# Two-layer RWKV-7 / neighbourhood-attention / retention step on one core: the next head pair's projections placed in the tail of a pair, its 64x64 inversion products on all four quadrants of TensorE

## What is computed

```python
h = rmsnorm(x, norm_mix_pre) * (1 + sc1) + sh1
z = h @ w_in                                   # 50 column tiles of 128; 40 of them belong to the head pairs
z_rwkv = dwconv3(z[..., :o0], rwkv_conv)       # three-tap convolution over time
r, k, v, wl, al, gl = split(z_rwkv)
kk = k * k_k;  kk = kk / max(sqrt(sum(kk * kk)), 1e-12)
decay = exp(-exp(w_log));  a = sigmoid(a0 + al @ a_up)
k_d = k * (1 + (a - 1) * k_a)
for t:                                         # both directions, per head
    S = S * w_t + (S a_t) b_t^T + v_t k_t^T;  y_t = S r_t
bonus = sum(r * k * r_k) * v
o = (head_groupnorm(y) * ln_g + ln_b + bonus) * g;  out_a = o @ w_o_rwkv
out_b = attention(q, k, v) @ w_o_na            # dense for the context, 8 x 16 neighbourhood for the latents
out_c = (head_groupnorm(retention(q, k, v)) * gn * silu(g)) @ w_o_ret
x = x + g1 * rmsnorm((gates * [out_a, out_b, out_c]).sum() @ w_out)
x = x + g2 * rmsnorm(conv_ffn(...))
```

## Time and profile before

| quantity | value |
|---|---|
| median of 3 runs | 2028.66 us (2023.75 to 2029.55) |
| the profiled execution's own time | 2028.39 us |
| its span | 2026.2 us |
| mean granted TensorE clock | 0.979 |
| busy: TensorE, VectorE, ScalarE, GpSimd | 93%, 50%, 46%, 47% |
| period of a pair (pair 1 to pair 2, layer 0) | 110.9 us |

### The profile page before, as it was taken

How to read it: one execution, slowest core, us unless ns; L and a number is a source line. 1 busy time by engine, 2 the same in 40 slices (tenths; PEclk the granted TensorE clock), 3 DMA queues, 4 the chain that set the end, 5 groups by cost and what they waited for, 6 DMA issues and landing times.

```text
span 2026.2 us, 41588 instructions
## 1 busy us (share of the span) xinstructions
PE 1890.5 (93%) x17864; PEld 1707.3 (84%) x17864; DVE 1005.3 (50%) x1516; ACT 939.4 (46%) x1766; POOL 942.6 (47%) x767
## 2 busy tenths in 40 slices
PE   5899999999999889999978999999999997999997
PEld 1887878787999779999948788787879996999996
DVE  3574756475612355551156566574655133455502
ACT  4554645454533454443355455453554334544432
POOL 1434435160666536666426052433516664466663
PEclk8999999999999989999989999999999999999998
DMA  7314142332443323334353241414224332234342
GB/s 291 104 53 147 55 133 79 111 102 88 136 125 125 104 73 124 121 123 126 132 214 107 62 131 55 136 55 135 77 98 147 124 125 83 94 125 125 125 125 73
DMA packets 65414, 231.52 MB, mean 114 GB/s; under 512 B 7376, under 2 KB 11856, under 8 KB 64592
## 3 DMA queue, kind: packets, MB, share of 16 engines
q1 hardware_dynamic: 59040, 215.21, 32.7%
q10 hardware_dynamic: 6192, 13.66, 1.9%
HBM read 223.58 MB, written 5.26 MB: 113 GB/s over the span
## 4 chain that ended last, share of the span: by engine, by line
PE 78%; DVE 11%; ACT 4%; issue 3%; POOL 2%; DMA 2%; ACTq 0%; SPq 0%; DVEq 0%; POOLq 0%
PE psz L471 55%; PE psw L471 20%; DVE work L1353 3%; ACT work L947 3%; DMA ring<-in_w 2%; DVE work L1362 2%; POOL ringlo L1728 1%; DVE part L1353 1%; PE psz L479 1%; ACT whi L947 1%; PE psw L479 1%; DVE rstd L1362 1%; DVE work L1356 1%; POOL work L1764 1%; DVE work L1359 0%
## 5 line engine op out<-in xcount | busy, mean ns | idle before, releaser
L1728 POOL TENSOR_TENSOR ringlo<-ring,whi 128x512 fp32r<-128x512 f32 x608 | 809.7, 1355 | 755.6 <-ACT whi L947 755.6
L471 PE MATMUL psz<-hhi,whi 128*128 128x386 f32 x1696 | 587.2, 346 | 23.2 <-POOL ringlo L1728 14.6
L471 PE MATMUL psz<-hlo,whi 128*128 128x386 f32 x1696 | 577.5, 340 | 0.0
L471 PE MATMUL psz<-hhi,ringlo 128*128 128x386 f32 x1696 | 576.3, 340 | 0.0
L947 ACT ACTIVATE whi<-ring 128x1024 fp32r<-128x1024 f32 x304 | 320.1, 1053 | 134.1 <-PE psz L471 125.7
L471 PE MATMUL psw<-work 64*64 64x64 f32 (+4 forms) x9024 | 347.5, 231 | 17.5 <-issue 9.0
L471 PEld LDWEIGHTS psw<-work 64*64 64x64 f32 (+2 forms) x9024 | 293.4, 136 | 72.1 <-issue 54.4
L471 PEld LDWEIGHTS psz<-hhi,whi 128*128 128x128 f32 x1696 | 320.9, 189 | 36.0 <-issue 18.6
L471 PE MATMUL psz<-part,whi 128*128 128x386 f32 x1344 | 346.6, 339 | 3.8 <-DVE work L1353 1.7
L471 PEld LDWEIGHTS psz<-hlo,whi 128*128 128x128 f32 x1696 | 322.9, 190 | 2.1
L471 PEld LDWEIGHTS psz<-hhi,ringlo 128*128 128x128 f32 x1696 | 321.1, 189 | 0.0
(11 more groups left out here) (105 smaller groups left out, 1700.6 us busy)
## 6 DMA issues: line engine op xcount, KB each, us to landing
ring<-in_w SPq DMA_DIRECT2D x400, 512.0 KB, 3.5
pk<-in_pk ACTq DMA_DIRECT2D x8, 832.0 KB, 4.5
const<-in_const SPq DMA_DIRECT2D x1, 1795.0 KB, 9.9
work<-in_x SPq DMA_DIRECT2D x1, 1544.0 KB, 6.8
work<-in_x ACTq DMA_DIRECT2D x1, 1544.0 KB, 9.0
out_x<-work ACTq DMA_DIRECT2D x1, 1544.0 KB, 5.6
work<-out_x ACTq DMA_DIRECT2D x1, 1544.0 KB, 8.8
out_x<-work SPq DMA_DIRECT2D x4, 386.0 KB, 2.4
```

The costliest lines, as they stand in the source:

```text
L471: ins = nc.tensor.matmul(out, a, b, start=start, stop=stop, skip_group_check=True)
L1728: L.do(G.tensor_tensor(out, a, b, op), S[sig] if sig else None)
```

## The change

What moves: the tiles r, k and v of pair p+1 are computed inside pair p (`next_steps`), 24 steps of three matmuls in eight groups from behind `wm`/`u` to the end of the pair. The stream of blocks in memory is the same; `ada_steps` moves forward, 14 of its 16 steps into levels 4 and 5. VectorE's `taps` of the next r, k, v and the new `key_tiles` follow in the tail, and `key_sums` opens the next pair, with nq behind it, then the low-rank products, nk, nv, rq. VectorE does `scale_rwkv` behind the scan of d = 0, `scale_ret` behind that of d = 1, and `finish` and the bonus behind the d-loop. GpSimd's `low` for rq and rk move into the loop's d = 0, behind `Lx` and behind the copies `pend`. The pair's parameters are loaded in two pieces (`load_ups`, `load_pack`). `Lx` and `Pi` get other buffers; `Px` holds the key norm.

In the levels hb = 1 takes the two other quadrants: its chunk operands `tvv`, `gg`, `g0`, `art` lie in the other half of the partitions, the loops run x outside and hb inside, and the waits ask for both heads. For it VectorE's transpose becomes one of 128 x 384 and two of 64 x 384 (`across`), and ScalarE's copy of `art` becomes three pieces.

```diff
-                        for i in range(p == 0, 5):
-                            dense(zb + i, bb + i)
+                        def next_steps(n):
+                            if p + 1 == PAIRS:
+                                return
+                            for _ in range(n):
+                                i, k = divmod(ahead[0], KT)
+                                zi, j = zb + ZI["r"] + i, bb + 10 + i
+                                if k == 0:
+                                    opened(zi)
+                                    pe.wait_ge(*after("w_lo", 2 * j + 2))
+                                three(z(zi), j, k, hsp[k], k == 0, k == KT - 1, "z_done" if k == KT - 1 else None)
+                                ahead[0] += 1
...
+                        else:
+                            key_sums()
+                            dense(zb + ZI["nq"], bb + 3)
                             pe.wait_ge(*at_of("yroot_ready", p - 1, 0))
                             pe.wait_ge(*at_of("rroot_ready", p - 1, 0))
+                            lora_up()
+                            dense(zb + ZI["nk"], bb + 4)
...
-                                    mm(psw[hc(c), hb, CH * x:CH * x + CH], au[hc(c), hb, x, 1, 0:CH],
+                                    mm(psw[hc(c ^ hb), hb, CH * x:CH * x + CH], au[hc(c), hb, x, 1, 0:CH],
...
-                                if lv == LEVELS - 1:
-                                    ada_steps(2)
+                                ada_steps(3 if lv == 4 else 4)
...
                         retain(2)
-                        ada_steps(4)
-                        freed(zb + 17)
-                        freed(zb + 18)
+                        ada_steps(2)
+                        next_steps(2)
...
-                        ada_steps(2)
+                        next_steps(3)
...
+                            else:
+                                split(sb_ + 10)
...
+                    def across():
+
+                        for c in range(2):
+                            flip(tvv[hc(1 - c), 1:2], xv[hc(c), 1:2], "tv_ready" if c else None)
...
-                                flip(tvv, xv, "tv_ready")
+                                flip(tvv[:, 0:1], xv[:, 0:1])
+                                across()
...
+                            if p:
+                                (scale_rwkv, scale_ret)[d](p - 1)
...
+                        if p:
+                            finish(p - 1)
+                        dve.wait_ge(*after("bon_done", p + 1))
+                        tt(bonus, w(1), vc, sig="bon_used")
...
-                        pool.wait_ge(*after("kk_sq", p + 1))
-                        low(sb_ + 6)
...
-                            if d:
-                                low(sb_ + 8)
+                            low(sb_ + (8 if d else 6))
```

More of the change, by code:

```diff
@@ new lines, in key_sums, with lora_up @@
+                        def key_sums():
+                            pe.wait_ge(*at_of("kk_sq", p, 0))
+                            mm(w(0), blk, tb, sig="kkn_done")
+                            pe.wait_ge(*at_of("kk_rk", p, 0))
+                            mm(w(1), blk, kd, sig="bon_done")
+                        def lora_up():
+                            pe.wait_ge(*after("lo_in", 16 * (p + 1)))
+                            lora = pk[:, PK["lora"]:PK["lora"] + 256]
+                            for d in range(2):
+                                mm(w(2 + d), lora[0:64, d * P:(d + 1) * P], lwal[0:64, :], sig="lw_done")
+                            for d in range(2):
+                                mm(w(4 + d), lora[64:128, d * P:(d + 1) * P], lwal[64:128, :], sig="la_done")
@@ new lines, in _ @@
+                        if p == 0:
+                            for i in (1, 2):
+                                dense(ZP + i, bb + i)
+                            dense(zb + ZI["nq"], bb + 3)
+                            dense(zb + ZI["nk"], bb + 4)
+                            key_sums()
+                            pe.wait_ge(*after("lora_in", 2))
+                            lora_up()
+                        else:
+                            key_sums()
+                            dense(zb + ZI["nq"], bb + 3)
@@ L693, in _ @@
+                        dense(zb + ZI["rq"], bb + 6)
                         pe.wait_ge(*after("pk_in", 16 * (p + 1)))
[L694 to L699 removed]
@@ L700, in _ @@
[L700 to L703 removed]
+                        turned(zb + ZI["nvt"], zb + ZI["nv"], mixed[1][p])
                         pe.wait_ge(*at_of("kkn_root", p, 0))
@@ L1073, in _, with query_in @@
-                        act.wait_ge(*at_of("kkn_done", p, 0))
-                        run(Pi, w(0), ACT.Sqrt, "kkn_root")
+                        if p == 0:
+                            for i, dst in enumerate((rc, kc_, vc)):
+                                centre_tap(dst, ZP + i, "conv", 4 * i)
+                                split(sb_ + i + 3)
+                        def query_in():
+                            seen(zb + ZI["nq"])
+                            run(nq, z(zb + ZI["nq"]), free=zb + ZI["nq"], scale=0.125)
+                            split(sb_ + 6)
@@ new lines, in key_in, with key_root @@
+                        def key_in():
+                            seen(zb + ZI["nk"])
+                            if p:
+                                act.wait_ge(*after("out_k", 32 * p))
+                            run(nk, z(zb + ZI["nk"]), free=zb + ZI["nk"])
+                            L.settle()
+                            act.dma_start(nak[layer, p], nk[:, 0:P]).then_inc(S["out_k"].h, 16)
+                            split(sb_ + 7)
+                        def key_root():
+                            act.wait_ge(*at_of("kkn_done", p, 0))
+                            run(Px, w(0), ACT.Sqrt, "kkn_root")
@@ L1226, in _ @@
                             run(u0[:, hb], six(w(2 + hb, 0, 384)), sig="u_ready")
+                        late_rows(p, zb + ZI["ada"])
+                        split(sb_ + 11)
                         for c in range(2):
@@ L1773, in _ @@
                             tt(ar[:, d, 1, :], rc, Pc, sig="rr_ready")
+                            if d:
+                                continue
+                            low(sb_ + 7)
+                            pool.wait_ge(*after("pk_in", 16 * (p + 1)))
+                            bias = pk[:, PK["bias"]:PK["bias"] + 768].rearrange("p (n c) -> p n c", n=12)
+                            tt(bias, bias, cv("colmask", 64).unsqueeze(1).to_broadcast([P, 12, 64]), ALU.add, sig="bias_ready")
                         low(sb_ + 9)
```

282 lines of the change are left out of this document (150 added, 132 removed).

## The result

The changed kernel took **2113.26 us** (median of 4 runs, 2108.71 to 2114.35); the kernel before, on the same chip, 2026.2 (4 runs, 2023.44 to 2029.55). The ratio is 1.042 (95% interval 1.0405 to 1.0435): 4.2% slower, 87 us, where 16 us had been forecast. The sign is right, the size is five times too small, and 2113 lies far above the range.

What follows compares the result with a forecast made beforehand. The prediction took TensorE as the bound almost everywhere. Levels 8 x 0, later heads less tails 6 x (4.1 - 3.9), first pairs 2 x 7.5, rest 0: 16 us on 2028.4, so 2044 us, range 2036 to 2056 (chance 0.52).

Steps and rivals of the forecast that it cites:

- part 3: Head of later pairs: 3 us stall at the second scores and smaller waits, 4.1 us lost a pair.
- part 1: Levels, all eight pairs: shorter four-quadrant products offset by bare copies, dearer transposes and a level-1 delay, about 0 a pair.
- part 2: Tail of six pairs: moved tiles fill waits, less a 2.1 us stall for r's low part; 3.9 us won a pair.
- part 4: Head of pair 0, twice: rq's low part 5.9 us late, further delays 1.6; 15.0 us lost for two layers.
- 3 won to 2 lost: Range in us given for the levels' sum per pair, around about 0.
- the bound of fixed cost: Levels, VectorE's three transposes: 0.6 us each if fixed cost ruled, 0.3 if half the partitions were half the work.
- Rival (a): Fill works, head holds: less GpSimd work beside VectorE, scores' stall 1 us, levels win 2; 2009 us, chance 0.20.
- The second part: Head of pair 0, later: rk's low part and the bias row delay others, rv's low part late; 1.6 us lost.
- Rival (c): TensorE loses its clock in the levels, adding 14 to 27 us: 2065 us; chance 0.11 together with (d).
- (d): Tail tiles delay the state chain instead of filling gaps, 3.4 us not won: 2065 us; chance 0.11 with Rival (c).

Runs made afterwards that it cites:

- e2: Changed kernel with GpSimd's order of before: rq's low part ahead of the loop, in first pairs also the bias row and rk's low part; 2094.7 us.
- e3: Kernel before with only the inversion products moved to four quadrants, with the extra transposes and the three-piece `art` copy; 2040.3 us.
- e7: e3 with the transposes across the halves moved behind VectorE's attention step in front of level 1; 2014.97 us.
- e14: e13 with ScalarE's split of the next pair moved behind the copies of u0 and the five steps in one piece; 2007.3 us.
- e13: e9 with the product on g_up and its copy moved behind the products and copies of g0; 2014.4 us.
- e11: Changed kernel with only the transposes across the halves moved behind the fourth scores; 2086.6 us.
- e1: Changed kernel with `finish` of the previous pair and the bonus product moved behind the first attention maximum on VectorE; 2078.1 us.
- e9: e4 with the transposes across the halves moved behind the fourth scores; 2030.3 us.
- e4: Changed kernel with the edits of e1 and e2, and `scale_rwkv` ahead of the first scan on VectorE; 2052.2 us.
- e8: e4 with the split behind the copies of u0, the five steps in one piece, and the transposes across behind the attention step; 2032.1 us.
- e12: e8 with the product on g_up placed earlier, between the projections rk and rv; 2021.7 us.

## Why the prediction was wrong, by its own steps

The step that failed is the later head (part 3): it forecast a stall of 3 us at the second scores, measured 7.8, six times, and had no term for the lower clock there. The levels (part 1), put at nothing, and the product on g_up, moved at no price in part 2, failed as well. The right sign is owed to part 4, which held 15 of the 16 us; parts 1 to 3 cancelled to 1 us in the forecast and together cost about 68, if the 19 us of e2 are taken for part 4.

**Part 1, the levels: the sum came out within its bounds only with another order of two calls.** "In level 1 the first attention maximum comes behind `across`, and ScalarE's exponential of it stands ahead of the `gg` copy: 1.2 us lost" named the place and the chain. The wait measured 2.1 us. What failed was to stop there: behind it TensorE ran at half clock through level 2. Its terms add up to 0.4 us a pair (the plain level's path to 5.55, not 5.4), and it wrote 0 for eight pairs; measured +13 us (e3), and -12 us (1.5 a pair, inside "3 won to 2 lost") with the order mended (e7). A product went from 1.61 to 0.93 us, 0.7 and not 0.8 less. The transposes: three of "about 0.55" are 1.78 us together in the plain levels, so half the partitions cost nothing less; the bound of fixed cost was the true one. The Trainium skill's rule (TensorEngine Tiling, PSUM Bottleneck) that tiling does not speed up the evacuation agrees with e7: of the 60 us that its products lost 12 show in the time, and 40.5 us of TensorE's waits are for the predicated copies that read them out of PSUM.

**Part 2, the tail: mechanism right, covered by a wait that was not in the sum.** The three waits of the earlier trace rows did vanish. The new stall for r's low part was 1.1 to 2.0 us, 1.6 in the mean, where 2.1 had been taken; but in four of the six tails 3.4 us at the lower level begin about where it ends, 1.7 us of work lost each, for which there was no term. Net 3.9 us a pair was too much, as far as it can be told: e14 against e7 is 7.6 us for six pairs, 1.3 a pair, but this holds the price of the head too, and e14 also has g_up and a split at places of their own; no run has the tail alone. The text moved g_up "away" at no price. TensorE stood 1.5 us in front of it in the changed kernel and 2.3 in each of six later heads once these were mended, and e13 shows 15.9 us for it; this is the step that is missing altogether.

**Part 3, the later head: the step that failed most.** "TensorE stalls 3 us at the second scores" was 7.8. The forecast's own terms give more than it wrote: 19.4 + 2.4 + 6.3 + 3.9 + 0.6 = 32.6 for VectorE, less 28.1, is 4.5 us. From `key_sums` on, TensorE's way came out nearly as forecast: it stood there from 355.09 - 7.82 - 317.80 = 29.5 us on, rv's wait of 1.4 included, against 28.1. VectorE's maximum came after 354.76 - 317.80 = 37.0 us, not 32. Its start was right (first scan 9.6 us behind `key_sums`, against 7.0 before: 2.5 later, forecast 2.4). The rest was mis-sized because the durations were taken from a head in which GpSimd did other work at other times: the second scan grew by 1.5 us, and the pairs of tensor operations from 1.02 to 3.22 and 3.16. From the first scan to the maximum it is 27.4 us, where the forecast had 22.9 (12.1 as before, and 10.8 of new work). So of the 4.8 us by which the stall was too small, 1.5 are the subtraction, and 3.3 are VectorE's longer operations less the 1.4 us by which TensorE itself came later. Rival (a) had the interaction the wrong way round: the change put more GpSimd work beside VectorE's chain, not less. And the lower clock, 19 us of work lost in the six heads, had no term.

**Part 4, pair 0: the large term right.** Forecast 5.9 us for rq, measured 5.73. The 15 us for two layers compare with 18.6 for undoing GpSimd's order everywhere (e2). The 18.6 us hold some lower clock too, which the forecast did not have (the first matmuls behind the 5.7 us wait take 0.53 us instead of 0.34). The second part had the wrong sign: the wait for rv's low part in pair 0 of layer 0 was 1.68 us before and 0.54 after, so it fell by 1.1 where 1.6 more had been taken.

**Rival (c)** had the price of one stretch right (3.4 us at the lower level, 1.7 lost) and its place in part. It expected the lower clock from gaps in the levels and gave it, with (d), 0.11. The traces show it at longer single waits: always at the 7.8 us ones, at the 2.1 us one of level 1 in all eight pairs of e3 but in six of eight in the changed kernel, and there at four of the six tails' waits of 1.1 to 2.0 us. e7's levels, pair 2, have seven waits of 0.3 to 1.7 us and full clock. A part that forecast a wait of some us should have had the lower clock as a bound; the earlier trace rows, read there as a curiosity of one tail, could have said so.

By size: late transposes 27 us (e11), `finish` and bonus 35 (e1), GpSimd's order 19 (e2). Added up, these make 80 of the 87, if they add; with `scale_rwkv` moved as well the three came to 83 (e9), and with g_up too the changed kernel is e13, 12 us under the kernel before. What `scale_rwkv` is worth alone was not run; e4 less e1 and e2 leaves 7 us for it and for what the two share. Open is also why the late split wins nothing on top of e4 and e9, yet 7 to 10 us once g_up has moved.

## What to carry to other kernels

Moving work into an engine's gaps takes away cover from whatever ran beside it at the old place: list that work, and read its durations beside the neighbours that it will have, not those it had. A new wait on TensorE of the sizes seen here (1.2 to 7.8 us) may bring the lower clock with it, and that belongs in the range: where it did, 3 to 7 us of work ran at half speed. The order of two calls on VectorE decided the sign of a change that makes products two fifths shorter. A change that bundles edits is worth taking apart: here three small ones cost 19 to 35 us each and hid what, with them and g_up's place mended, is a kernel 1% faster.

## What the runs showed of the hardware

- The granted clock fell at single waits, in the pair shown before they ended: in e3 at one of 2.1 us, in a stretch with 2.49 of 4.0 us busy (mean clock 0.57 over the 8 us that follow), in the changed kernel at one of 7.8 us (0.50 over the 7 us behind it). With the wait at 0.7 us (e7) it stayed at 1.00. The same 2.1 us wait left it at 1.00 in two of eight pairs of the changed kernel, and waits of 1.2 to 2.0 us in its tails had 3.4 us at the lower level beside them in four of six, so the wait's length alone does not tell.
- At the lower level a product of 48 records took 1.56 us instead of 0.93, and a dense matmul of 386 columns 0.53 instead of 0.34.
- A transpose of 64x384 on VectorE took 0.57 us in the mean, as much as one of 128x384 (0.58; 1.78 us for the level's three).
- A VectorE scan took 0.96 us alone and 2.46 beside a GpSimd operation, ending 0.81 us behind it.
- The moved kernels vary more from run to run than the kernel before: e8 over 2018.4 to 2035.1, e12 over 2011.3 to 2033.5, where the kernel before stays within 2021.6 to 2032.3 beside all the experiments. Their half clock varies with them (mean clock 0.969 to 0.976 in e8's runs).
